# Four unused tiles are allocated, which shifts where the tiles that TensorE reads begin

## The chip, the cores and the metric

The kernel runs on one core of one Trainium2 chip. The metric is the device time of one launch in microseconds (us), the median of several runs. Times of single instructions are in nanoseconds (ns).

## What is computed

Two network blocks in float32, one after the other, on a sequence of 1024 positions with 1024 channels. Cut to what matters:

```python
# first block
h = rms_norm(x, norm_mix_pre)
proj = h @ w_in                                 # feeds four mixers of 256 channels each:
o_a = gated_delta_rule(...)                     # chunks of 64, 4 heads
o_b = block_sweep_attention(...)                # latent attention
o_c = gla_chunked(...)                          # gated linear attention
o_d = block_sweep_attention(..., forget_cum)    # forgetting attention
for i in range(4):
    gate = sigmoid(h @ w_gate[i] + b_gate[i])   # 4 x (1024 x 1024)
    merged = merged + gate * (branches[i] @ w_branch_up[i])
x = x + rms_norm(merged @ w_out, norm_mix_post)
h2 = rms_norm(x, norm_mlp_pre)
u = relu(h2 @ w_mlp_in)                         # 1024 -> 4096
x = x + rms_norm((u * u) @ w_mlp_out, norm_mlp_post)
# second block
proj = h @ w_in_2                               # 1024 -> 11 x 512
...                                             # recurrence, three convolutions, pooling
y = cat @ w_out_2                               # 2048 -> 1024
return rms_norm(x + gate * y, final_g)
```

The large products take most of the arithmetic.

## The kernel before

Channels lie on the 128 partitions, positions run along them. A large product is done by `gemm` (line 125) in units: one unit is 128 output channels for all 1024 positions, with the weights of that unit loaded to `weights_raw` (two slots). Float32 precision is made from two parts. ScalarE rounds the weights to a high part in `weights_parts` (line 234), VectorE subtracts it from the raw weights and leaves the low part beside it (line 250). The activations are split in the same way into a tile that holds both parts (`hidden`, `mlp_in`, `mixer_in`, `branches`, `mixed_parts`, `glu_parts`). TensorE then multiplies high by high, high by low and low by high, each for two halves of 512 positions:

```python
for wp, xp in ((0, 0), (0, 1), (1, 0)):
    for h in range(halves):
        mm = nc.tensor.matmul(c.psum[:, bank + h, 0:cols],
                              c.parts[:, s, wp, at], moving(k, xp, h), ...)
```

That is line 283. The first operand, `weights_parts`, is stationary: TensorE loads 128 columns of it. The second is streamed, 512 columns in a product. A unit over 1024 input channels has 8 x 3 x 2 = 48 such products. In the trace's names, as in psum<-mixer_in,weights_parts, the streamed tile stands first and the stationary one second.

The same products appear at other lines. Line 453 multiplies gate weights with `hidden` in portions of three, put between the small steps of the mixers (`EarlyGates`). Line 324 and a few more start a product in another order. At lines 2698 (`mlp_rows`) and 2936 (`merged_rows`) the roles are turned: the activations (`mixer_in` or `mlp_in`) are stationary and weights are streamed, partly from `weights_parts`, and partly from `out_weights` or from the room of `mlp_in`. Transposes stream `identity`. The delta rule (`delta_net_chunks`, line 1120) multiplies blocks of 64x64 in plain float32, for instance at line 1464.

TensorE waits for VectorE's low part of a unit (semaphore `low_ready`) and for the PSUM banks of two units back. SyncE loads the weights of a unit as soon as the low part two units before has been made. The order of the work on each engine is written out in the source.

Tiles are allocated by `Core.sb`. Those on the left side are stacked upward in each partition, in the order of the calls, and a closed context gives its room back. Those on the right are stacked down from the upper end. The stack on the left, with the bytes that each tile takes of a partition: `weights_raw` (8192), `weights_parts` (16384), `identity` and `all_ones` (512 each), `vectors` (349 numbers, 1396), `epsilon` (8), `mod_times` and `mod_plus` (64 each), `mod_gate` (32), then `hidden` (65536), and above it the tiles of the mixers. After the mixers `mlp_in` takes the place of `hidden`, with `gate` (16384) and `branches`, or `out_weights`, above it; later `pool_projected` (32768) begins there, with `glu_parts` or `mixed_parts` above. Where the stack begins, and whether a size is rounded up, is not in the source. On the right are `branch_plain`, in its place later `y` (32768 bytes each), and under `y` `mixer_in` (65536).

Of the kernel before, what the change touches and what calls it, by code (L numbers as in the profile page):

```python
# [20 lines left out]
P = 128  # L21
# [6 lines left out]
HEADS, DH = 4, 64  # L28
CH = 64
# [10 lines left out]
class Steps:  # L40
# [4 lines left out]
    def __init__(self, c, engine, spec):  # L45
        self.c, self.engine, self.sem, self.base = c, engine, c.steps[engine], c.base[engine]
        self.at, self.count, self.order, n = {}, {}, [], 0
        for item in spec:
            what, k = item if isinstance(item, tuple) else (item, 1)
            turns = (what,) if isinstance(what, str) else what  # L50
            for m, name in enumerate(turns):
                assert name not in self.at, name
                self.at[name], self.count[name] = (n + m + 1, len(turns)), k
            self.order += list(turns) * k
            n += k * len(turns)
        self.n, self.next = n, 0
# [26 lines left out]
class Core:  # L83


    def __init__(self, nc, ctx):
        self.nc, self.ctx, self.used = nc, ctx, {}
        self.steps = {e: self.sem(f"{e}_steps") for e in ("pe", "act", "vec", "pool", "dma")}
        self.base = {e: 0 for e in (*self.steps, "gemm_act", "gemm_dve")}
        self.loaded = [self.sem(f"weights_loaded_{s}") for s in range(2)]  # L90
        self.high_ready = self.sem("high_part_ready")
        self.low_ready = self.sem("low_part_ready")
        self.unit_done = self.sem("unit_multiplied")
        self.act_done = self.sem("unit_evacuated_by_act")
        self.dve_done = self.sem("unit_evacuated_by_dve")
        self.units = 0
        self.loads = [0, 0]
        self.ahead = None
        self.raw = self.sb("weights_raw", [P, 2, WK * P])
        self.parts = self.sb("weights_parts", [P, 2, 2, WK * P], F32R)  # L100
        self.psum = ctx.enter_context(nc.psum_tensor("psum", [P, 8, HALF], F32))
        self.scratch_stored = self.sem("scratch_stored")
        self.stored = 0
        self.slot_stored = [self.sem(f"slot_stored_{s}") for s in range(2)]
        self.slots = [0, 0]
        self.residual_loaded = [self.sem(f"residual_loaded_{n}") for n in range(2)]
        self.residuals = [0, 0]
        self.ctx_loaded = self.sem("ctx_loaded")
# [4 lines left out]
    def sb(self, name, shape, dtype=F32, ctx=None, side="left"):  # L113

        self.used[name] = self.used.get(name, 0) + 1
        if self.used[name] > 1:
            name = f"{name}_{self.used[name]}"
        return (ctx or self.ctx).enter_context(self.nc.sbuf_tensor(name, shape, dtype,
                                                                    side=side))
# [604 lines left out]
def project(nc, c, weights, first, n_units, hidden, out, then=None, act_epilogue=None,  # L724
            **options):


    def evacuate(act, u, s, result, act_count, dve_count, q, j):
        nc.scalar.copy(out[:, bass.ds(u, 1), :].rearrange("p a n -> p (a n)"),
                       result).then_inc(c.act_done, 1)  # L730
    gemm(nc, c, weights, n_units, KT, lambda k, part, h: hidden[:, k, part, h * HALF:(h + 1) * HALF],
         act_per_unit=1, act_epilogue=act_epilogue or evacuate, first=first, then=then, **options)
# [187 lines left out]
def delta_net(nc, c, t, hidden, small, early, merged_ctx):  # L920

    with ExitStack() as ctx:
        proj = c.sb("dn_projected", [P, 8, S], ctx=ctx)
        o_tok = c.sb("dn_out_tokens", [P, BLK + 1, 256], ctx=ctx)
        with ExitStack() as inner:
            padded_rows = c.sb("dn_rows", [P, S + P], ctx=inner)
            rows = padded_rows[:, 0:S]
            g_tok = c.sb("dn_decay_tokens", [P, BLK, HEADS], ctx=inner)
            masks = c.sb("dn_masks", [P, DN_MASKS, CH], ctx=inner)
            select = c.sb("dn_row_selectors", [P, 10, P], ctx=inner)  # L930
            project(nc, c, t["w_in"], 2, 8, hidden, proj, early.then())
            early.begin(14, hidden,
                        lambda half: 7 if 8 <= half < 25 else 6 + half % 2, (t["w_in"], 10, KT))
            delta_net_inputs(nc, c, t, proj, rows, g_tok, small, padded_rows, masks, select, early)
            delta_net_chunks(nc, c, t, proj, padded_rows, g_tok, o_tok, masks, select, early)
        plain = c.sb("branch_plain", [P, 4, 2, S], ctx=merged_ctx, side="right")
        tokens_to_channels(nc, c, o_tok[:, 1:, :], plain[:, 0], early, 26, proj[:, 6:8, :],
                           vec(c, "dn_norm"))
        early.end()
    return plain  # L940
# [179 lines left out]
def delta_net_chunks(nc, c, t, proj, rows, g_tok, o_tok, masks, select, early):  # L1120
# [5 lines left out]
    with ExitStack() as ctx:  # L1126
        def sb(name, *shape):
            return c.sb("dn_" + name, [P, *shape], ctx=ctx)
        ks, qs, kb, kbe, kt, vb = (sb(n, 2, P) for n in
                                   ("k", "q", "k_beta", "k_beta_decay", "k_tail", "v_beta"))  # L1130
        twice = lambda *a: (sb(*a), sb(*a))
        qds, all_ends, qks = twice("q_decay", 2, P), twice("chunk_decay", 2, 2), \
            twice("qk_turned", HEADS, CH)
        dec_t, dec = sb("decay_turned", HEADS, CH), sb("decay", HEADS, CH)
        a_t, a_0 = sb("a_turned", HEADS, CH), sb("a", HEADS, CH)
        a_lev = sb("a_levels_turned", LEVELS - 1, HEADS * CH)
# [1619 lines left out]
def branches(nc, c, t, merged_ctx):  # L2756

    with ExitStack() as ctx:
        hidden = c.sb("hidden", [P, KT, 2, S], F32R, ctx=ctx)
        norm_input(nc, c, t, hidden)  # L2760
        with ExitStack() as inner:
            small = c.sb("small_projections", [P, 2, S], ctx=inner)
            early = EarlyGates(nc, c, t, inner)
            project(nc, c, t["w_in"], 0, 2, hidden, small, (t["w_in"], 2, KT))
            plain = delta_net(nc, c, t, hidden, small, early, merged_ctx)
            latent_attention(nc, c, t, hidden, small, early, plain[:, 1])
            gated_linear(nc, c, t, hidden, small, early, plain[:, 2])
            forgetting_attention(nc, c, t, hidden, small, early, plain[:, 3])
    return plain, early
# [1064 lines left out]
def build(nc, t):  # L3834
    with ExitStack() as ctx:
        c = Core(nc, ctx)
        scratch = {"x_mid": [P, BLK, D], "x_second": [P, BLK, D],
                   "cat": [4 * MIX, P, S], "gate": [32, P, S]}
        for name, shape in scratch.items():
            t[name] = nc.dram_tensor(f"{name}_scratch", shape, F32, kind="Internal").ap()  # L3840
        load_constants(nc, c, t)
        merged_ctx = ctx.enter_context(ExitStack())
        times, plus = c.sb("mod_times", [P, KT, 2]), c.sb("mod_plus", [P, KT, 2])
        gate = c.sb("mod_gate", [P, KT])
        plain, early = branches(nc, c, t, merged_ctx)
        with ExitStack() as mlp_ctx:
            h = c.sb("mlp_in", [P, KT, 2, S], F32R, ctx=mlp_ctx)
            gate_and_merge(nc, c, t, plain, early, h)
            merged_rows(nc, c, t, plain[:].rearrange("p i t s -> p (i t) s"), h)
            merged_ctx.close()  # L3850
            y = c.sb("y", [P, KT, S], side="right")
            mix_ctx = ctx.enter_context(ExitStack())
            mixer_in = c.sb("mixer_in", [P, KT, 2, S], F32R, ctx=mix_ctx, side="right")
            mlp(nc, c, t, h, y, mixer_in, (times, plus, gate))
            mlp_rows(nc, c, t, y, h, mixer_in, times, plus)
        project_and_recur(nc, c, t, mixer_in, y, times, plus)
        with ExitStack() as tiles_ctx:
            tiles = c.sb("pool_projected", [P, 2 * MIX, S], ctx=tiles_ctx)
            two_convolutions(nc, c, t, mixer_in, y, tiles)
            x_ctx, final_ctx = ctx.enter_context(ExitStack()), ctx.enter_context(ExitStack())  # L3860
            pooling = glu_conv_branch(nc, c, t, mixer_in, mix_ctx, y, tiles, x_ctx)
            mixer_out(nc, c, t, y, tiles, pooling, x_ctx, final_ctx, gate)
# [191 lines left out]
```

## Time and profile before

| | |
|---|---|
| median of 3 runs | 2975.11 us (2971.45 to 2978.17) |
| the profiled execution, its own time | 2972.37 us |
| its span, first to last instruction | 2970.5 us |
| TensorE busy | 2774.9 us, 93% |
| weight loads, beside the products | 2163.1 us, 73% |
| VectorE busy | 1390.4 us, 47% |
| ScalarE busy | 968.4 us, 33% |
| GpSimd busy | 124.3 us, 4% |
| mean granted TensorE clock | 0.974 of 2.4 GHz |
| memory traffic over the span | 72 GB/s |

The span is about 2 us shorter than the device time of the same execution. PE is TensorE, PEld its weight loads, DVE VectorE, ACT ScalarE, POOL GpSimd. Products of TensorE overlap in its pipeline: the time of one in a row of groups is longer than the distance between two. The distance is had from the timeline, where a row is a run of like instructions with its start and its length; the length reaches to the end of the last one, some 0.39 us after that one's start.

### The profile page before, as it was taken

The page shows a single profiled execution, that of the slowest core. Times are in us where ns is not written, and L with a number is a line of the kernel's source. Part 1 is how long each engine was busy: PE and PEld are TensorE (multiplying, and loading weights), DVE is VectorE, ACT ScalarE, POOL GpSimd, SP SyncE. Part 2 cuts the span into 40 slices and gives each one's busy share as a digit, 9 for nine tenths or more (in the row PEclk, how much of TensorE's full clock was granted, in tenths as well). Part 3 has the DMA queues.
Part 4 walks back from the last instruction along what each step waited for, and adds up shares of the span by engine and source line. Part 5 has one row for each costly group of instructions (what it writes and reads, how often), then busy time and mean ns, then how long its engine had stood idle before and what let it go on. Part 6 is the DMA issues. An engine that isn't in the chain of part 4 may idle for free. (4 is left out here: it accounts for less than half of the span.)

```text
span 2970.5 us, 35094 instructions
## 1 busy us (share of the span) xinstructions
PE 2774.9 (93%) x14780; PEld 2163.1 (73%) x14780; DVE 1390.4 (47%) x1696; ACT 968.4 (33%) x1377; POOL 124.3 (4%) x191
## 2 busy tenths in 40 slices
PE   6999998899978989989999999998999899998996
PEld 5867776666756766778888888887777678867775
DVE  2164443344133234954434334235556688833933
ACT  3142212244122344543323223124455521223022
POOL 0001110000000200100010111000000000000000
PEclk9989999999999999999999999999999999999998
DMA  2121011210111111641232333113211111113231
GB/s 103 43 74 41 30 34 40 68 33 29 46 60 58 43 39 58 219 183 71 86 99 85 107 96 101 45 43 135 78 36 57 43 58 56 50 50 125 71 127 71
DMA packets 68199, 214.63 MB, mean 72 GB/s; under 512 B 8040, under 2 KB 12936, under 8 KB 68048
## 3 DMA queue, kind: packets, MB, share of 16 engines
q1 hardware_dynamic: 52784, 158.72, 16.3%
q0 software_dynamic: 15264, 53.75, 5.4%
q8 instruction: 113, 1.85, 0.3%
q14 instruction: 38, 0.31, 0.0%
HBM read 176.78 MB, written 35.65 MB: 72 GB/s over the span
## 5 line engine op out<-in xcount | busy, mean ns | idle before, releaser
L283 PE MATMUL psum<-mixer_in,weights_parts 128*128 128x512 f32 x3168 | 754.0, 399 | 22.4 <-PEq L186 15.5
L283 PEld LDWEIGHTS psum<-mixer_in,weights_parts 128*128 128x128 f32 x3168 | 598.4, 189 | 169.8 <-issue 17.7
L453 PE MATMUL psum<-hidden,weights_parts 128*128 128x512 f32 x1536 | 436.1, 426 | 32.9 <-ACT early_gate L477 14.6
L453 PEld LDWEIGHTS psum<-hidden,weights_parts 128*128 128x128 f32 x1536 | 288.2, 196 | 116.6 <-issue 31.4
L250 DVE TENSOR_TENSOR weights_parts<-weights_raw,weights_parts 128x1024 fp32r<-128x1024 f32 (+2 forms) x173 | 184.4, 1066 | 349.0 <-ACT weights_parts L234 349.0
L283 PE MATMUL psum<-mlp_in,weights_parts 128*128 128x512 f32 x1440 | 330.4, 392 | 0.4 <-DVE weights_parts L250 0.4
L283 PEld LDWEIGHTS psum<-mlp_in,weights_parts 128*128 128x128 f32 x1440 | 270.6, 188 | 59.8 <-DVE weights_parts L250 0.9
L283 PE MATMUL psum<-hidden,weights_parts 128*128 128x512 f32 x1200 | 278.4, 394 | 8.8 <-PEq L647 3.4
L283 PEld LDWEIGHTS psum<-hidden,weights_parts 128*128 128x128 f32 x1200 | 227.1, 190 | 59.8 <-issue 6.9
L234 ACT CAST weights_parts<-weights_raw 128x1024 fp32r<-128x1024 f32 (+2 forms) x173 | 159.7, 923 | 328.6 <-PE psum L283 254.7
L3393 DVE SCALAR_TENSOR_TENSOR y<-y,vectors 128x1009 f32<-128x1009 f32 (+14 forms) x120 | 153.1, 1276 | 3.3
L283 PE MATMUL psum<-mixed_parts,weights_parts 128*128 128x512 f32 x576 | 134.9, 396 | 0.7 <-DVE weights_parts L250 0.7
L283 PEld LDWEIGHTS psum<-mixed_parts,weights_parts 128*128 128x128 f32 x576 | 108.4, 188 | 26.5 <-issue 3.0
L2432 DVE TENSOR_SCALAR squares<-psum 128x1024 f32<-128x1024 f32 x32 | 39.2, 1225 | 146.8 <-PE psum L283 139.6
L283 PE MATMUL psum<-branches,weights_parts 128*128 128x512 f32 x384 | 94.7, 404 | 6.7 <-DVE branches L2295 4.0
L2425 ACT ACTIVATE squares<-squares 128x1024 f32<-128x1024 f32 x32 | 33.9, 1060 | 190.7 <-DVE squares L2432 190.7
L283 PEld LDWEIGHTS psum<-branches,weights_parts 128*128 128x128 f32 x384 | 72.0, 193 | 29.2 <-DVE weights_parts L250 9.5
L2444 DVE TENSOR_TENSOR y<-y,psum 128x1024 f32<-128x1024 f32 x16 | 19.5, 1220 | 118.6 <-PE psum L283 118.6
L789 ACT ACTIVATE mod_weights<-mod_weights 128x512 f32<-128x512 f32 x80 | 49.9, 624 | 77.3 <-DVE mod_weights L797 77.3
L2435 DVE TENSOR_TENSOR mixer_in<-squares,mixer_in 128x1024 fp32r<-128x1024 f32 x32 | 39.2, 1225 | 72.8 <-ACT mixer_in L2427 72.8
L2936 PE MATMUL psum<-out_weights,mlp_in 128*128 128x512 f32 x288 | 70.2, 399 | 3.1 <-DVE out_weights L2889 3.1
L2698 PE MATMUL psum<-mlp_in,mixer_in 128*128 128x512 f32 x288 | 71.7, 399 | 0.0
(470 smaller groups left out, 3269.0 us busy)
## 6 DMA issues: line engine op xcount, KB each, us to landing
weights_raw<-in_w_in SPq DMA_DIRECT2D x69, 512.0 KB, 3.6
weights_raw<-in_w_mlp SPq DMA_DIRECT2D x56, 512.0 KB, 3.5
mod_weights<-in_mod_w POOLq DMA_DIRECT2D x80, 256.0 KB, 3.8
weights_raw<-in_w_gate SPq DMA_DIRECT2D x32, 512.0 KB, 3.7
gate_scratch<-early_gate SPq DMA_DIRECT2D x64, 256.0 KB, 2.0
gate<-gate_scratch POOLq DMA_DIRECT2D x32, 512.0 KB, 3.8
weights_raw<-in_w_out SPq DMA_DIRECT2D x20, 512.0 KB, 3.6
x_tokens<-in_x SPq DMA_DIRECT2D x4, 1024.0 KB, 8.2
```

The costliest lines, as they stand in the source:

```text
L234: nc.scalar.copy(c.parts[:, s, 0, 0:w], c.raw[:, s, 0:w]).then_inc(c.high_ready, 1)
L250: nc.vector.tensor_tensor(c.parts[:, s, 1, 0:w], c.raw[:, s, 0:w], c.parts[:, s, 0, 0:w].bitcast(F32), ALU.subtract).then_inc(c.low_ready, 1)
L283: mm = nc.tensor.matmul(c.psum[:, bank + h, 0:cols], c.parts[:, s, wp, at], moving(k, xp, h), start=(n < halves), stop=(n >= halves * (3 * ...
L453: mm = nc.tensor.matmul(c.psum[:, bank, :], c.parts[:, s, wp, at], self.hidden[:, k, xp, h * HALF:(h + 1) * HALF], start=(k == 0 and n == ...
L789: self.nc.scalar.activation(w, w, ACT.Copy, accum_out=self.sums[:, h, n, x:x + 1]).then_inc(self.act.step(f"summed{m}"), 1)
L2425: nc.scalar.activation(sq[:, s, :], sq[:, s, :], ACT.Square).then_inc(c.act_done, 1)
L2432: nc.vector.tensor_scalar(sq[:, s, :], result, 0.0, None, ALU.max).then_inc(c.dve_done, 1)
L2435: nc.vector.tensor_tensor(u_parts[:, k, 1, :], sq[:, s, :], u_parts[:, k, 0, :].bitcast(F32), ALU.subtract).then_inc(c.dve_done, 1)
L2444: nc.vector.tensor_tensor(y[:, k, :], y[:, k, :], result, ALU.add).then_inc(c.dve_done, 1)
L2698: last = mm(ps[:, 2 * (b % 2) + n, :], hidden[:, k, xp, columns(b)], weights(k, wp)[:, n * HALF:(n + 1) * HALF], start=(k == 0 and xp == 0 ...
L2936: last = mm(ps[:, 2 * (b % 2) + n, :], h[:, k, xp, columns(b)], weights(k, wp)[:, n * HALF:(n + 1) * HALF], start=(k == 0 and xp == 0 and ...
L3393: stt(at, x[:, max(0, s):S - max(0, -s)], w, at, ALU.mult, ALU.add).then_inc(vecs.step(f"tap{n}"), 1)
```

## The change

Four tiles are allocated that no instruction reads or writes: 28 bytes at the bottom of the left stack, 32 bytes at the top of the right one, 32 bytes within the delta rule's tiles, and 36 bytes below `hidden`. They are named for what they are to give: that each tile read by TensorE begins at a multiple of 64 bytes in its partition. The instructions of every engine, their order and their operands by name are the same as before.

```diff
--- before.py
+++ after.py
@@ -96,6 +96,8 @@
         self.units = 0
         self.loads = [0, 0]
         self.ahead = None
+        self.sb("first_tile_at_64_bytes", [P, 7])
+        self.sb("right_tile_at_64_bytes", [P, 8], side="right")
         self.raw = self.sb("weights_raw", [P, 2, WK * P])
         self.parts = self.sb("weights_parts", [P, 2, 2, WK * P], F32R)
         self.psum = ctx.enter_context(nc.psum_tensor("psum", [P, 8, HALF], F32))
@@ -1129,8 +1131,9 @@
         ks, qs, kb, kbe, kt, vb = (sb(n, 2, P) for n in
                                    ("k", "q", "k_beta", "k_beta_decay", "k_tail", "v_beta"))
         twice = lambda *a: (sb(*a), sb(*a))
-        qds, all_ends, qks = twice("q_decay", 2, P), twice("chunk_decay", 2, 2), \
-            twice("qk_turned", HEADS, CH)
+        qds, all_ends = twice("q_decay", 2, P), twice("chunk_decay", 2, 2)
+        sb("tiles_at_64_bytes", 8)
+        qks = twice("qk_turned", HEADS, CH)
         dec_t, dec = sb("decay_turned", HEADS, CH), sb("decay", HEADS, CH)
         a_t, a_0 = sb("a_turned", HEADS, CH), sb("a", HEADS, CH)
         a_lev = sb("a_levels_turned", LEVELS - 1, HEADS * CH)
@@ -3842,6 +3845,7 @@
         merged_ctx = ctx.enter_context(ExitStack())
         times, plus = c.sb("mod_times", [P, KT, 2]), c.sb("mod_plus", [P, KT, 2])
         gate = c.sb("mod_gate", [P, KT])
+        c.sb("hidden_at_64_bytes", [P, 9])
         plain, early = branches(nc, c, t, merged_ctx)
         with ExitStack() as mlp_ctx:
             h = c.sb("mlp_in", [P, KT, 2, S], F32R, ctx=mlp_ctx)
```

## Rows read from the trace of the kernel before

**Rows 1.** The page, part 1, and the list of cores: busy time and granted clock.

```profile
PE 2774.9 (93%) x14780; PEld 2163.1 (73%) x14780; DVE 1390.4 (47%) x1696; ACT 968.4 (33%) x1377; POOL 124.3 (4%) x191
...
core 0: 2970.5 us, clock 0.974
```

**Rows 2.** Window 2400 to 2600: PE, PEld, DVE, ACT, POOL busy (instructions), granted clock, DMA.

```profile
2400.00:2600.00 200.00, 200.00 (x859) 160.96 (x858) 176.19 (x143) 44.38 (x44) 1.61 (x3) 1.00 0.17 53
```

**Rows 3.** Timeline of TensorE, 1561 to 1827 us: start, length, then the run.

```profile
1561.54 88.06 PE L283 MATMUL psum<-mlp_in,weights_parts 128*128 128x512 f32 x384
1649.44 89.76 PE L283 MATMUL psum<-mixer_in,weights_parts 128*128 128x512 f32 x384
1739.04 88.06 PE L283 MATMUL psum<-mlp_in,weights_parts 128*128 128x512 f32 x384
```

**Rows 4.** Timeline of TensorE, 1292 to 1308 us, line 2936.

```profile
1292.56 1.56 PE L2936 MATMUL psum<-weights_parts,mlp_in 128*128 128x512 f32 x6
1293.96 13.78 PE L2936 MATMUL psum<-out_weights,mlp_in 128*128 128x512 f32 x60
```

**Rows 5.** Timeline of TensorE from 2022 us, line 2698.

```profile
2022.38 14.16 PE L2698 MATMUL psum<-mlp_in,mixer_in 128*128 128x512 f32 x60
```

**Rows 6.** Groups of TensorE by line and form: busy us, mean ns | idle before.

```profile
L283 PE MATMUL psum<-mixer_in,weights_parts 128*128 128x512 f32 x3168 | 754.0, 399 | 22.4 <-PEq L186 15.5 <-DVE weights_parts L250 6.9
L453 PE MATMUL psum<-hidden,weights_parts 128*128 128x512 f32 x1536 | 436.1, 426 | 32.9 <-ACT early_gate L477 14.6 <-POOL gla_state L1700 8.5 <-PEq L1692 3.6
L283 PE MATMUL psum<-mlp_in,weights_parts 128*128 128x512 f32 x1440 | 330.4, 392 | 0.4 <-DVE weights_parts L250 0.4
L283 PE MATMUL psum<-hidden,weights_parts 128*128 128x512 f32 x1200 | 278.4, 394 | 8.8 <-PEq L647 3.4 <-PEq L839 2.8 <-PEq L186 1.4
L283 PE MATMUL psum<-mixed_parts,weights_parts 128*128 128x512 f32 x576 | 134.9, 396 | 0.7 <-DVE weights_parts L250 0.7
L283 PE MATMUL psum<-branches,weights_parts 128*128 128x512 f32 x384 | 94.7, 404 | 6.7 <-DVE branches L2295 4.0 <-DVE weights_parts L250 1.8
L2698 PE MATMUL psum<-mlp_in,mixer_in 128*128 128x512 f32 x288 | 71.7, 399 | 0.0
L2936 PE MATMUL psum<-out_weights,mlp_in 128*128 128x512 f32 x288 | 70.2, 399 | 3.1 <-DVE out_weights L2889 3.1
L324 PE MATMUL psum<-mixed_parts,weights_parts 128*128 128x512 f32 x192 | 47.7, 412 | 11.5 <-DVE mixed_parts L2375 11.5
L2226 PE MATMUL psum<-identity,attention_probs 128*128 128x128 f32 x288 | 43.7, 279 | 7.0 <-ACT attention_probs L2113 6.7
...
L1464 PE MATMUL psum<-dn_inverse,dn_a_levels_turned 64*64 64x64 f32 x640 | 27.3, 225 | 0.0
L2936 PE MATMUL psum<-weights_parts,mlp_in 128*128 128x512 f32 x96 | 26.6, 428 | 3.9 <-PEq L186 3.6 <-DVE row_work L2910 0.3
L2698 PE MATMUL psum<-weights_parts,mixer_in 128*128 128x512 f32 x96 | 26.4, 426 | 2.8 <-DVE row_slots L2655 2.8
...
L283 PE MATMUL psum<-glu_parts,weights_parts 128*128 128x512 f32 x96 | 22.2, 393 | 1.4 <-PEq L186 1.4
```

**Rows 7.** A window (columns as in rows 2) and the timeline, at a granted clock of 0.50.

```profile
1178.00:1181.00 3.00, 3.00 (x8) 2.32 (x8) 2.47 (x3) 2.91 (x3) 0.00 (x0) 0.50 0.96 373
...
1177.21 5.03 PE L283 MATMUL psum<-branches,weights_parts 128*128 128x512 f32 x11 [4.00 <-DVE branches L2295]
```

**Rows 8.** Groups of ScalarE's casts and of VectorE's low parts.

```profile
L234 ACT CAST weights_parts<-weights_raw 128x1024 fp32r<-128x1024 f32 x138 | 144.7, 1048 | 291.6 <-PE psum L283 228.4 <-DMA weights_raw<-in_w_in 20.0 <-PE psum L324 17.7
...
L2427 ACT CAST mixer_in<-squares 128x1024 fp32r<-128x1024 f32 x32 | 33.5, 1048 | 1.0
...
L2370 ACT CAST mixed_parts<-pool_projected 128x1024 fp32r<-128x1024 f32 x8 | 7.7, 1041 | 0.0
...
L3525 ACT CAST glu_parts<-y 128x1024 fp32r<-128x1024 f32 x4 | 3.9, 1052 | 0.0
...
L250 DVE TENSOR_TENSOR weights_parts<-weights_raw,weights_parts 128x1024 fp32r<-128x1024 f32 x138 | 168.6, 1222 | 332.1 <-ACT weights_parts L234 332.0
```

## The prediction

> **What bounds the kernel now.** I read the page first: TensorE is busy for 2774.9 of 2970.5 us, VectorE for 1390.4, ScalarE for 968.4 [rows 1]. A busy TensorE proves little, so I took a window where VectorE is densest: there TensorE is busy for all 200 us and VectorE for 176 only [rows 2]. In the timeline, runs of 384 products stand end to end with no idle between them [rows 3]. The end of the kernel comes when the stream of 128x512 products has gone through. What a product costs is therefore what its successor must wait, start to start, and not the 390 to 400 ns that the grouped rows print, which overlap.
>
> The timeline gives that spacing cleanly, since whole runs of one kind follow each other without idle. Between the starts of neighbouring runs of 384 products lie 87.90 us for mlp_in (1561.54 to 1649.44) and 89.60 us for mixer_in (1649.44 to 1739.04) [rows 3]: 228.9 and 233.3 ns a product, same line, same shape, same clock, same instruction order. A run of 60 out_weights products takes 13.78 us with the last one's 0.39 in it: 13.39/59 = 227.0 ns. Six products that stream weights_parts against the same stationary mlp_in start 1.40 us before their successor: 233.3 ns [rows 4]. With mixer_in stationary and mlp_in moving, 60 products take 14.16 us: (14.16 - 0.40)/59 = 233.2 ns [rows 5]. So four pairs of tiles have three rates, though all do the same arithmetic.
>
> **Where the tiles begin.** Modulo 64, let weights_raw begin at b. From the sizes in the source, weights_raw and weights_parts are multiples of 64 bytes, so weights_parts is at b. Up to hidden come identity, all_ones (512 each), vectors (1396), epsilon (8), the mod tiles (64 + 64 + 32): hidden is at b + 8192 + 16384 + 1024 + 1396 + 8 + 160 = b + 27164, which is b + 28. mlp_in takes hidden's place later, and out_weights, branches and mixed_parts lie whole multiples of 64 above it. mixer_in is stacked down from the right end. So before the change the stationary weights and the streamed activations differ in phase by 28 bytes, if tiles are packed without rounding. The change puts weights_parts at b + 28 and hidden at b + 28 + 28 + 36 = b + 92, again b + 28: **weights_parts comes into the phase that hidden, mlp_in and out_weights have already**, and those keep theirs. mixer_in moves by 32. The description says that this phase is a multiple of 64, which makes b = 36 and mixer_in's present start 32.
>
> Read with these starts, the rates have an order. Both operands at 0: 227.0 (out_weights, mlp_in). Streamed one at 0, weights_parts at 36: 228.9. Streamed one off (mixer_in at 32, weights_parts at 36): 233.3, in both cases. One exception in size: streamed at 0 with mixer_in stationary at 32 costs 233.2 and not 228.9. I can't say why 32 should hurt a stationary operand more than 36; but nothing at 227 is off, and everything off is above it.
>
> **The change part by part.** No instruction is added, removed or moved on any engine; the tiles are written by nobody. There is no new wait and no new transfer. What changes is start addresses, and I price these by the row of the pair that has both at 0, 227.0. Counts are from the groups [rows 6] (first units of a product have lines of their own, under 200 products more; left out, they are worth under 1 us):
> - mixer_in streamed, weights_parts stationary: 3168, 6.3 ns each: 20.0 us.
> - mlp_in, hidden, mixed_parts, branches, glu_parts streamed at lines 283 and 324: 1440 + 1200 + 576 + 384 + 192 + 96 = 3888, 1.9 ns each: 7.4 us.
> - hidden at line 453: 1536 at 1.9 ns: 2.9 us. They are laid three at a time between the small products of the delta rule and the attentions, so part of this ends in a wait for VectorE or ScalarE; I count half, 1.5, and keep 0 and 2.9 for the range.
> - line 2698, one operand off in all: 288 + 96 = 384 at 6.3: 2.4 us. Line 2936 with weights_parts streamed: 96 at 6.3: 0.6 us. Its 288 with out_weights are at 227.0 already: nothing.
>
> Sum: 31.9 us, with the first units 32.5. From it goes what runs at the lower clock. There 11 products take 5.03 us at a granted clock of 0.50, which is 1.2 GHz [rows 7]: 430 to 450 ns each, near the 427 ns of 512 columns at that clock, so a few ns more for an operand are hidden in it, and I give these products no gain. A mean granted clock of 0.974 makes 5.2% of the span low: 1.7 us off. **31 us** are left, rounded. All of it lies on the path where TensorE never waits [rows 2, 3].
>
> Transposes stream identity, which moves from 36 to 0. No row shows one with both operands aligned. Bounds: none of them gains, or each of them gains 1.9 ns, 288 in the largest group [rows 6]; with the others, some 800, 1.5 us. They stand in short groups at the ends of waits, nearer to nothing: 0. The float32 products of 64x64 run on chains through VectorE and ScalarE: 0, with a bound of 1.9 ns on the 640 of line 1464 [rows 6] and two more groups of that kind and size, some 1900, 3.6 us, and as much to the other side, since their tiles move by 32 bytes too.
>
> ScalarE's casts into weights_parts and mixer_in take 1048 ns, those into mixed_parts 1041 [rows 8]. That may be worth 7 ns on 170 casts, 1.2 us. It is hidden: ScalarE and VectorE make the weights a unit ahead, and VectorE waits 332 us for casts [rows 8] while TensorE waits for neither in the middle. If that cover were gone it would be those 1.2 us. With TensorE faster, a unit of 48 shrinks from 11.2 to 10.9 us; in 2400 to 2600 VectorE has 176.2 us of work for what would then be 194.5 us [rows 2]. The cover holds, with 9% to spare. What is late next is nothing new.
>
> Against its own time the profiled execution (2972.4 us, span 2970.5) would go to 2941; the median of the runs shown is 2.7 us above it, so 2975.1 - 31 = **2944 us**.
>
> **The rivals.**
> - *A finer grain than 64 bytes.* mixer_in's 32 would then be a good start already, weights_parts' 36 a bad one, and mixer_in's 4.4 ns over mlp_in has another cause, such as its place at the far end of the partition. Only weights_parts gains: 3168 + 3888 + 1536 = 8592 at 1.9 ns, and 96 streamed at 6.3: 16.9 us, less the low clock and half of line 453: 15 us, 2960. For it: no row has mixer_in at another start. Against: weights_parts streamed from the near end costs the same 233.3, and one step of 33 in place of 32 pieces of 64 bytes would be 227.0 x 33/32 = 234.1, close to the 233.3 seen. The Trainium skill, "SBUF — State Buffer", section "Specifications (TRN2)", gives SBUF cachelines of 16 bytes with a penalty for each cross to a new line; by it, 32 is a line's start and 36 is not, and this rival would be the outcome; the rows above do not agree with it, since mixer_in at 32 has the slowest rate. Chance 0.10.
> - *The stack rounds every tile up to 32 bytes* (28 becomes 32, 36 becomes 64, epsilon's 8 becomes 32). Then weights_parts and hidden both begin at a multiple of 64 now, and the change puts both at 32; only mixer_in gets better. The price: the 3888 + 1536 products with an aligned streamed operand go from 228.9 to 233.3, 23.9 us; 288 out_weights products lose 6.3, 1.8 us; mixer_in's stay at 233.3, since one operand of two is off as before. 25.7 us less the low clock: slower by 24, 2999. It decides as soon as hidden and mlp_in leave their phase. Against it: weights_parts and out_weights would have the same phase now, yet streamed against the same tile they take 233.3 and 227.0 [rows 4], and the casts into weights_parts go with those into mixer_in, not with those into mixed_parts [rows 8], though glu_parts at 1052 blurs that. For it: the pair at 32 that breaks my order of rates. Chance 0.07.
> - *The change does nothing for the end.* The rates are not of the start, but of which tiles meet (distance in the partition, banks). Then all pairs keep theirs: 2975. For it: 32 and 36 as stationary starts that differ by 4.4 ns. Chance 0.05.
>
> **How the numbers follow.** Forecast 0.76 (in it that half of a term goes astray); finer grain 0.10; rounding 0.07; nothing 0.05; something else below the forecast 0.02. The bounds of the unknown terms are 31 + 1.4 + 1.5 + 3.6 = 37.5 and 31 - 1.5 - 3.6 = 26 us, so the forecast's own range is 2938 to 2949, and 3 us more on each side for the spread of the runs. To reach 8 in 10 with the second case in it, the range goes from 2934 to 2961; rounding and nothing stay outside, with a little at each end. A measurement of this kernel can tell about 0.2%, 6 us, from no change. Faster: 0.76 + 0.10 + 0.02, less 0.01 for a gain that drowns: 0.87. Within 0.2%: 0.06. Slower: 0.07.
>
> **What the changed profile would show.** Runs of 384 mixer_in products with starts 87.1 to 87.3 us apart in place of 89.60, and of mlp_in 87.1 to 87.3 in place of 87.90, so that both kinds become alike; six weights_parts products before the next out_weights ones at 1.36 us in place of 1.40; counts and order of instructions as before; casts into weights_parts near 1042 ns. Mixer_in at 89.6 or 89.0 with mlp_in at 87.2 would be the first rival; mlp_in at 89.6 the second, and that would make the prediction wrong in sign. If both kinds become alike and the time still falls by under 20 us, the loss must stand as new idle time of TensorE, most likely at line 453.

## The result and the profile after

The changed kernel takes **2986.49 us** (median of 7 runs, 2983.86 to 2987.44) against 2975.11 us before (7 runs, 2971.16 to 2979.31). The ratio is 1.0036, with a 95% interval of 1.0025 to 1.0048: it is slower by 11 us. 2944 us had been forecast, and the range ended at 2961.

The page of the changed kernel, parts 1 and 5. Its line numbers are 2 higher than before from line 99 on, and 3 higher from 1134 on:

```profile
span 2985.6 us, 35094 instructions
...
PE 2795.2 (94%) x14780; PEld 2164.3 (72%) x14780; DVE 1391.3 (47%) x1696; ACT 969.4 (32%) x1377; POOL 124.5 (4%) x191
...
L285 PE MATMUL psum<-mixer_in,weights_parts 128*128 128x512 f32 x3168 | 753.6, 398 | 22.7 <-PEq L188 15.6
...
L285 PE MATMUL psum<-mlp_in,weights_parts 128*128 128x512 f32 x1440 | 336.1, 395 | 0.4 <-DVE weights_parts L252 0.4
...
L285 PE MATMUL psum<-hidden,weights_parts 128*128 128x512 f32 x1200 | 283.7, 398 | 8.8 <-PEq L649 3.4
```

TensorE is busy 20.3 us longer for the same 14780 instructions [rows 1], and the other engines as long as before, within 1 us. Of that, mlp_in has 5.7 us and hidden 5.3 at line 283's products, and hidden at line 453 has 4.2 (440.3 against 436.1); mixer_in has -0.4 [rows 6]. In total TensorE's idle time has not grown: it is 190.4 us, against 195.6 before. So some 5 us of the 20 fell where TensorE waits anyway, and the profiled span grew by 15.1 us. The medians are only 11.4 apart. Part of the difference is the clock: the mean granted clock of the profiled execution was 0.974 before and is 0.972 here.

The timeline of TensorE, for the stretch of [rows 3]; columns are start, length, run:

```profile
1566.53 89.39 PE L285 MATMUL psum<-mlp_in,weights_parts 128*128 128x512 f32 x384
1655.76 89.77 PE L285 MATMUL psum<-mixer_in,weights_parts 128*128 128x512 f32 x384
1745.37 89.76 PE L285 MATMUL psum<-mlp_in,weights_parts 128*128 128x512 f32 x384
1834.96 89.76 PE L285 MATMUL psum<-mixer_in,weights_parts 128*128 128x512 f32 x384
```

Runs of mixer_in stand 89.61 us apart (1655.76 to 1745.37), as before. Those of mlp_in went from 87.90 to 89.23 and 89.59. Both kinds have become alike, at the slow rate: 232.4 to 233.3 ns a product. And line 2936, for [rows 4]:

```profile
1296.46 1.55 PE L2939 MATMUL psum<-weights_parts,mlp_in 128*128 128x512 f32 x6
1297.85 13.78 PE L2939 MATMUL psum<-out_weights,mlp_in 128*128 128x512 f32 x60
```

out_weights against mlp_in is at (13.78 - 0.39)/59 = 227.0 ns, to the digit what it was. Whatever the pads did to mlp_in's start, they did to that of out_weights as well, and this pair did not mind.

In the program as built every left tile is rounded up to 32 bytes. From weights_parts to hidden lie 19008 bytes before: the sizes named ahead of the prediction, with 1408 for 1396 and 32 for 8. These are the starts in bytes, with what they leave modulo 256, and below them the distances of the tiles that meet in a product (streamed start less stationary start):

| | before | the change |
|---|---|---|
| weights_parts | 24704 (128) | 24736 (160) |
| hidden, mlp_in | 43712 (192) | 43808 (32) |
| out_weights | 109248 (192) | 109344 (32) |
| mixer_in | 131040 (224) | 131008 (192) |
| distance modulo 256: hidden or mlp_in to weights_parts | 64 | 128 |
| mixer_in to weights_parts | 96 | 32 |
| out_weights to mlp_in | 0 | 0 |
| weights_parts to mlp_in | 192 | 128 |
| mlp_in to mixer_in | 224 | 96 |

Before, all but mixer_in were at multiples of 64 already. The change puts mixer_in there and takes the others off. With these starts the row of out_weights speaks against every theory in which each operand's own start modulo 64 sets the rate: both of its operands went from a multiple of 64 to 32 beyond one, and it cost nothing.

### The profile page after: what moved, and what is told of

It is laid out like the page before. It is cut to its first block and busy times, and to the rows that moved or that the text cites. A ratio compares the mean times of both kernels' runs of the same rounds, so it can differ in the third digit from the quotient of the medians.

```text
span 2985.6 us, 35094 instructions
## 1 busy us (share of the span) xinstructions
PE 2795.2 (94%) x14780; PEld 2164.3 (72%) x14780; DVE 1391.3 (47%) x1696; ACT 969.4 (32%) x1377; POOL 124.5 (4%) x191
## 5 line engine op out<-in xcount | busy, mean ns | idle before, releaser
L455 PE MATMUL psum<-hidden,weights_parts 128*128 128x512 f32 x1536 | 440.3, 428 | 32.2 <-ACT early_gate L479 14.4
L285 PE MATMUL psum<-hidden,weights_parts 128*128 128x512 f32 x1200 | 283.7, 398 | 8.8 <-PEq L649 3.4
L479 ACT COPY early_gate<-psum 128x512 f32<-128x512 f32 x64 | 37.4, 586 | 102.2 <-PE psum L455 102.0
```

The source lines that it names most:

```text
L285: mm = nc.tensor.matmul(c.psum[:, bank + h, 0:cols], c.parts[:, s, wp, at], moving(k, xp, h), start=(n < halves), stop=(n >= halves * (3 * ...
L455: mm = nc.tensor.matmul(c.psum[:, bank, :], c.parts[:, s, wp, at], self.hidden[:, k, xp, h * HALF:(h + 1) * HALF], start=(k == 0 and n == ...
L479: nc.scalar.copy(self.out[:, h, :], c.psum[:, self.bank(2 * u + h), :]).then_inc(self.copied, 1)
```

## The experiments

The theories of the expectations: **A**, each operand's own start counts, in a grain of 64 bytes; **B**, the distance between the streamed and the stationary start counts. Four runs went first, one with products alone and three with single pads. The kernel before was timed again beside them: 2975.62 us beside the first three kernels with pads, 2974.73 us beside the later ones.

**Products alone, at chosen starts.** The core of the kernel, where `at` gives the numbers at a byte address of one large tile:

```python
for m, w, how in starts():
    for i in range(4):
        mm(65536, 24576, 128)          # 128 columns: marks where a new pair begins
    for dm, dw in how:
        last = mm(m + dm, w + dw)      # streamed start, stationary start, 512 columns
```

> Leaves out the whole computation: only 128x512 products of float32r, streamed and stationary operand at chosen starts in one big tile, 27 fixed pairs of starts (30 products each) and 12 runs of 96 in the order of a matrix product. It measures the disputed cost by itself. Theory A (each operand's own start counts, in a grain of 64 bytes): the pair at multiples of 64 takes 227 ns a product, every streamed start off by 4 to 48 bytes 233.3, starts off by 64, 128, 256 ... again 227. Theory B (the distance of the two starts counts): moving both by the same 4 to 64 bytes leaves the rate as it was, and moving one by 64, 128 or more can change it although both stay multiples of 64. The run with hidden's and weights_parts' present addresses (43712, 24704) should repeat 228.9 and the one with mixer_in's (131040, 24704) 233.3 under both.

Timeline of TensorE in four windows of this kernel: distance 0, 64, 128, and 256 bytes. The marks are merged with the rest, so windows were laid inside the runs:

```profile
67.78 4.47 PE L78 MATMUL psum<-big 128*128 128x512 f32 x19
...
104.64 4.74 PE L78 MATMUL psum<-big 128*128 128x512 f32 x20
...
119.64 4.60 PE L78 MATMUL psum<-big 128*128 128x512 f32 x19
...
126.84 4.47 PE L78 MATMUL psum<-big 128*128 128x512 f32 x19
```

(4.47 - 0.39)/18 = 226.7 ns, (4.74 - 0.39)/19 = 228.9, (4.60 - 0.40)/18 = 233.3, and 226.7 again (the last product of a window is 0.39 or 0.40 us long). The second and third have both starts at multiples of 64, and are slow: A fails. Moving both by 32 or by 64 left 226.7, as B wants. Moving both by 4 gave 237.8 and by 16 gave 231.1, which B did not expect: it holds for starts at multiples of 32 alone. The kernel's own pairs were repeated: 228.8 for hidden's and weights_parts' addresses, 233.3 for mixer_in's, 232.4 for the change's hidden. Nothing else ran on the core then, so neither ScalarE, VectorE nor a transfer has a part in it.

**The right pad alone.**

```diff
+        self.sb("right_pad", [P, 8], side="right")
         self.raw = self.sb("weights_raw", [P, 2, WK * P])
```

> Only the 32 bytes at the right end. If tiles are rounded up to 32 bytes and the left stack begins at a multiple of 64, as the run of the change suggests, this alone puts every tile of the products at a multiple of 64. Theory A: mixer_in's products go from 233.3 to 228.9, 3168 x 4.4 ns less the low clock, 13 us: 2962. Theory B: the distance of mixer_in and weights_parts becomes 64 modulo 128, the one of hidden and weights_parts now, so it expects the same 228.9 and 2962. If neither holds, 2975.

Measured: 2961.11 us, ratio 0.9945 (0.9932 to 0.9958). This is what the change describes, every such tile at a multiple of 64, and it is 14 us faster than before. The timeline agrees: runs of mixer_in now stand 87.9 us apart, as those of mlp_in do. This run can't tell A from B.

**The first left pad alone.**

```diff
+        self.sb("first_pad", [P, 8])
         self.raw = self.sb("weights_raw", [P, 2, WK * P])
```

> Only 32 bytes at the bottom of the left stack: weights_parts, hidden, mlp_in and the rest of the left side all begin at 32 modulo 64, as in the change, and mixer_in stays at 32. Theory A: every product has its operands off, 5400 products go from 228.9 to 233.3, 24 us less the low clock: 2998. Theory B: hidden and weights_parts keep their distance, 228.9, and mixer_in comes to 64 modulo 128 from weights_parts, so its products fall to 228.9: 2962.

Measured: 2962.83 us, ratio 0.9954 (0.9942 to 0.9967). That is within 1 us of what B said, where A wanted 2998. Every one of these tiles is off a multiple of 64 here, and the kernel gains nearly as much (13 us) as with all of them on one (14). Its timeline:

```profile
1563.19 88.06 PE L283 MATMUL psum<-mlp_in,weights_parts 128*128 128x512 f32 x384
1651.09 88.06 PE L283 MATMUL psum<-mixer_in,weights_parts 128*128 128x512 f32 x384
```

**64 bytes below hidden alone.**

```diff
+        c.sb("hidden_pad", [P, 16])
         plain, early = branches(nc, c, t, merged_ctx)
```

> Only 64 bytes below hidden: hidden, mlp_in, out_weights, branches, mixed_parts move by 64, weights_parts and mixer_in stay. Theory A: all starts keep their value modulo 64, so nothing changes: 2975. Theory B: the distance of hidden and weights_parts goes from 64 to 0 modulo 128, as in the change, where their products took 232.4 to 233.3: 5400 x 4 ns, less the low clock and what waits cover at line 453: 16 to 20 us slower, 2993.

Measured: 2985.39 us, ratio 1.0032 (1.002 to 1.0043). No start changes modulo 64, and the change's loss is there: 10 us of its 11. The sign is B's, the size about half of the 18 us that B had said. The rates are as B had them; what failed is how much of them reaches the end. At 1561 us before, with some 3400 of the 5400 dearer products done, this kernel is only 5.1 us behind (1561.54 to 1566.67, below), where 3400 at 4 ns would make 14. In the delta rule's stretch, from the row of line 1503 at 259.54 us to that at 487.31, it loses nothing (227.77 us before, 227.68 here), with 336 products of line 453 in it. So in the first block most of the loss does not reach the end, as it would if it fell where TensorE waits for the small steps of the mixers; which waits take it up was not followed. In the long runs after 1561 us, where TensorE never waits [rows 2, 3], the loss counts in full: the profiled span ends another 9 us later, and the 2000 products left at 4.4 ns make 9.

```profile
1566.67 89.76 PE L283 MATMUL psum<-mlp_in,weights_parts 128*128 128x512 f32 x384
1656.27 89.77 PE L283 MATMUL psum<-mixer_in,weights_parts 128*128 128x512 f32 x384
```

The next four asked how B goes on, and whether it can be used.

**Products alone, distances from 0 to 480.** The kernel above with other starts.

> Again only products at chosen starts, the computation left out. Streamed minus stationary start from 0 to 480 bytes in steps of 32, for stationary starts of 0, 32 and 128 modulo 256; then both off by 4, 8, 16, 64, 128 bytes at distance 0; small distances; and four runs of 192 in the product's order at distances 0, 64, 128, 192. Theory B, as the first run of pairs left it: for starts at multiples of 32 the rate depends on the distance modulo 256 alone: 226.7 ns at 0 and 256, 228.8 at 64, 232.4 to 233.3 at 128, 233.3 at 192, 233 to 234 at all odd multiples of 32, the same for the three stationary starts. Theory A is out for multiples of 32 if the rows at distance 0 are 226.7 at a start of 32 too. What it can't say beforehand: whether 320, 384 and 448 repeat 64, 128 and 192; the theory says they do.

For multiples of 32 all of it came out so. Start to start, means over each run of 30 once it has settled (its first products, up to ten, still differ): 226.7 at 0 and 256; 228.9 at 64 and 320; 232.1 to 232.7 at 128 and 384; 233.2 to 233.3 at 192 and 448; 233.2 to 234.3 at the odd multiples of 32; the same for stationary starts at 0, 32 and 128. The four long runs, at distances 0, 64, 128 and 192:

```profile
504.83 40.52 PE L76 MATMUL psum<-big 128*128 128x512 f32 x178
...
548.83 40.45 PE L76 MATMUL psum<-big 128*128 128x512 f32 x176
...
593.69 40.60 PE L76 MATMUL psum<-big 128*128 128x512 f32 x174
...
638.77 40.53 PE L76 MATMUL psum<-big 128*128 128x512 f32 x173
```

In 40.5 us go 178, 176, 174 or 173 products: (40.52 - 0.39)/177 = 226.7 and (40.53 - 0.40)/172 = 233.3 ns. Below 32 bytes the starts themselves count too: both off by 4 at distance 0 gave 237.8, both off by 8 231.0, by 16 229.9. There the distance doesn't set the rate either: a distance of 240 gave 226.7 with the stationary start off by 16 (run pairs_1), and 236.8 with the streamed one off. Tiles are rounded to 32 bytes, so the kernel never meets that.

**All distances at multiples of 256.**

```diff
+        self.sb("right_pad", [P, 24], side="right")
         self.raw = self.sb("weights_raw", [P, 2, WK * P])
...
+        c.sb("hidden_pad", [P, 48])
         plain, early = branches(nc, c, t, merged_ctx)
```

> 192 bytes below hidden and 96 at the right end: weights_parts, hidden, mlp_in, out_weights, branches, mixed_parts, glu_parts and mixer_in all begin at 128 modulo 256, so every distance is a multiple of 256. Theory B: all products at 226.7: 3168 x 6.6 + 3888 x 2.1 + 1536 x 2.1 (half of it in waits) + 384 x 6.6 + 96 x 6.6 = 33.8 us, less the low clock: 32 us faster, 2943. A theory in which only multiples of 64 matter expects what the right pad alone gave, 2961.

Measured: **2948.28 us**, ratio 0.991 (0.9895 to 0.9925), 26 us faster than before and 38 faster than the change. It beats both kernels.

```profile
1552.23 87.20 PE L283 MATMUL psum<-mlp_in,weights_parts 128*128 128x512 f32 x384
1639.27 87.20 PE L283 MATMUL psum<-mixer_in,weights_parts 128*128 128x512 f32 x384
...
2355.97 219.79 PE L283 MATMUL psum<-mixer_in,weights_parts 128*128 128x512 f32 x960 [12.05 <-PEq L186]
```

Both kinds are at 87.04 us for 384, 226.7 ns. The 960 products of the convolutions are at 219.4/959 = 228.8 ns on average, but not because they wait. Their first ten fall into 4.13 us at a granted clock of 0.51; the gaps there are 426 or 427 ns. This is the window of the rest (columns as in [rows 2]):

```profile
2360.10:2575.00 214.90, 214.90 (x950) 177.91 (x949) 192.75 (x156) 46.38 (x46) 1.92 (x4) 1.00 0.17 53
```

TensorE is busy for all of it, the mean gap is 226.7 ns, and VectorE is busy for 90%. So VectorE's cover holds at the best rate too. Over the whole kernel TensorE's waits for VectorE's low parts (line 250), summed over the five largest groups of line 283, went from 9.8 to 12.1 us.

The 5 us to the expected 2943 are in part the clock. The profiled execution has a mean granted clock of 0.971 against 0.974, some 16 us more at the low level. Of the 18 executions of the kernel before, the three at 0.970 took 2979.1 to 2980.0 us and the three at 0.975 or 0.976 took 2970.9 to 2971.5: about 1.5 us for 0.001. By this estimate the clock makes 4 to 5 us between the two profiled executions, and some 2 between the medians (mean clocks 0.9726 before, 0.9715 here). The remaining 3 us or so of the medians are not traced to a place. Line 453 is not it: its group gave 2.0 us (436.1 to 434.1), where 1.6 had been counted. Whether the faster stream itself draws more of the low clock, no run separates.

**192 bytes below hidden alone.**

> The 192 bytes below hidden alone, mixer_in left at 32 modulo 64. Theory B: the 3888 products of line 283 and 324 go from 228.8 to 226.7, 8.2 us, line 453 gives 1.6, weights streamed at line 2936 0.6; mixer_in stays at a distance of 96 modulo 256: 10 us faster, 2966. A theory of multiples of 64: 2975.

Measured: 2965.24 us, ratio 0.9969 (0.9957 to 0.998), as B had said. mlp_in's runs take 87.24 us, mixer_in's 89.78.

**The change without its pad below hidden.**

```diff
-        c.sb("hidden_at_64_bytes", [P, 9])
         plain, early = branches(nc, c, t, merged_ctx)
```

> The change without its pad below hidden. weights_parts 160, hidden 224, mixer_in 192 modulo 256. Theory B: hidden and weights_parts are 64 apart again, 228.8, and mixer_in is 32 from weights_parts, 233.3: the rates of before and its time, 2975, so that the pad below hidden carries the whole loss of the change. If the starts themselves mattered (weights_parts and hidden at 32 modulo 64) it would be slow like the change, 2986.

Measured: 2974.61 us, ratio 1.0 (0.9991 to 1.0009, 11 runs). Runs of mlp_in and mixer_in stand 87.91 and 89.59 us apart, as before. So the other three pads come to nothing together, and 36 bytes, rounded up to 64, carry the whole loss. The first left pad and the right pad each gained 13 to 14 us alone; together they leave mixer_in 32 bytes from weights_parts, at the slow rate again. The delta rule's pad was not tried alone.

**Products with two pairs of starts in turn.** B is a rule, not a mechanism. One more run asked which of the loads a product's stream has to be far enough from.

> Products alone again, the computation left out. Which distance counts: that of a product to its own stationary operand, or to the one that is loaded for the next product while this one streams? 60 products take two pairs of starts in turn. Theory B1 (own pair): (0,0) and (64,64) in turn stay at 226.7 ns; (64,0) and (0,64) in turn lie between the rates of 64 and 192, near 231. Theory B2 (the load beside it): (0,0) and (64,64) in turn, where the load beside is 64 or -64 away, give near 231, and (64,0) and (0,64) in turn, where the load beside is at distance 0, give 226.7; the same with 128 and 32. Both expect 226.7, 228.8, 232.4, 233.3 for the constant pairs at 0, 64, 128, 192.

The timeline: (0,0) throughout, (0,0) and (64,64) in turn, (64,0) and (0,64) in turn:

```profile
68.78 10.59 PE L81 MATMUL psum<-big 128*128 128x512 f32 x46
...
82.65 10.59 PE L81 MATMUL psum<-big 128*128 128x512 f32 x45
...
139.66 10.66 PE L81 MATMUL psum<-big 128*128 128x512 f32 x45
```

226.7, (10.59 - 0.39)/44 = 231.8 and (10.66 - 0.39)/44 = 233.4 ns. Own pairs at distance 0 don't suffice (B1 wanted 226.7 for the second), nor does a neighbouring load at distance 0 (B2 wanted 226.7 for the third). Both theories fall. Each has a part in it, though. (128,0) and (0,128) in turn, with own distances of 128 and the neighbouring load at 0, ran at 230.0 ns (46 products in 10.74 us), where 128 throughout gave 232.4; (32,0) and (0,32) in turn ran at 230.0 too, where 32 throughout gave 233.3. These are faster than the own distances alone allow, so the neighbouring load counts; they are slower than 226.7, so the own distance counts as well. (0,0) and (128,128) in turn, with own distances of 0 and the neighbouring load at 128, ran at 228.3. Among starts at multiples of 32 the best rate was seen only with all of them, own and neighbouring, at a common value modulo 256. How the two parts add up can't be told from these runs.

## Why the prediction was wrong

- **The bound** was right: TensorE's stream of products. 20 us more in it gave 15 in the profiled span and 11 in the medians.
- **The rates** were read right: 227.0, 228.9, 233.3. Experiments with nothing but products repeat each within 0.3 ns.
- **The step that failed is "Where the tiles begin".** It put hidden 28 bytes in phase from weights_parts "if tiles are packed without rounding". They are rounded, weights_parts and hidden both began at multiples of 64, and the change did not bring them together but from a distance of 64 to one of 128 modulo 256. So the products with hidden and mlp_in went from 228.9 to 232.4 to 233.3 ns where the sum had them fall to 227.0, and those with mixer_in stayed at 233.3 (distance 96, then 32) where it had them fall by 6.3 ns and gain 20 us. I let the description of the change fix the phase (b = 36), and made the rates fit it.
- **The exception was the clue.** A stationary operand at 32 that costs 4.4 ns more than one at 36 stood there as something that I couldn't explain, and I went on. With the starts as built the pairs of tiles at multiples of 64 had three rates, 227.0, 228.9 and 233.3, in one and the same trace; no rule of single starts can give that. I had taken just this as proof against rounding, by which I kept theory A and gave up the addresses, where it was the other way round.
- **The rival of rounding** had the right sign and the right layout (chance 0.07), and 24 us in place of 11. One of its terms was false: out_weights stayed at 227.0. Another was too large: of what line 453 and line 283's products with hidden and branches lost in the first block, most did not reach the end. It was built on A too.
- **The rival "which tiles meet (distance in the partition, banks)"** had the mechanism (0.05), but its forecast of no change was careless: I wrote that all pairs keep their rates, and the pad below hidden changes a distance by 64.
- **The price of the best pair** was right, and so the forecast's size came true for another kernel: all distances at multiples of 256 gave 2948 us, where 2944 had been said for this one. That is no support for the argument: the layout that earns it is not the one that the prediction took for the best.
- **The rival of a finer grain** is out: 32 bytes decide nothing by themselves, and multiples of 64 are not alike.
- The casts of ScalarE that I had used against rounding (1048 ns into weights_parts, 1041 into mixed_parts) show no phase: in the changed kernel those into mixer_in take 1050 at a multiple of 64 and those into glu_parts 1046 off one.
- The cover of VectorE held: at 226.7 ns a product TensorE still goes without a gap through the convolutions, with VectorE busy for 90% there.

## What to carry to other kernels

When products of TensorE stream 512 numbers of float32r and load a new stationary operand each time, compare start to start per pair of tiles, and lay out tiles by their distance modulo 256 bytes (starts at multiples of 32 are what was measured): it was worth 3% per product and 1.3% of this kernel between the change's layout and the best one. Read start addresses from the built program and not from sizes in the source, and where one pair of tiles breaks the rule that the others suggest, don't price anything by that rule until it is explained. Padding every tile to a round address is not a gain in itself: 32 bytes in one place won 14 us here, 64 in another lost 10.

## What the runs showed of the hardware

- A product of 512 columns with its own load of 128 columns took from 226.7 to 237.8 ns, start to start, at a granted clock of 1.0 and with every other engine at rest, by start addresses alone. At a granted clock of 0.50 it is 426 to 428 ns, before (mixer_in and weights_parts 96 apart) as with all distances at multiples of 256, so no difference by address was seen there.
- The rate is that of a repeating pattern, not of single products: at distance 64 the gaps go 226, 229, 232 ns and again; at 128 seven gaps of 228 to 241 ns repeat. The same addresses can settle in two patterns: two runs of mlp_in in the changed kernel took 89.23 and 89.59 us from start to start, and one pair at distance 128 (65664 and 24576) ran at 233.5 ns in pairs_1 and 232.4 in pairs_2.
- The Trainium skill, "TensorE: Matmul & The Clock Gate", section "Step-by-step: what each phase is for", says that the streamed operand and the weight load have SBUF read ports of their own, and that loading the next weights takes no read bandwidth from the running product. With the addresses of either operand alone unchanged modulo 256, the other's move by 64, 128 or 192 bytes cost 2 to 7 ns a product here. These runs do not agree with full independence: the two do meet somewhere. Where, no run shows.
